# An encoder block with a mixture of experts: router logits with the router's weights as the stationary side, token numbers inside the first expert product, masks on GpSimd

## What is computed

```python
h = rms_norm(x, norm1_g);  z = h @ w_in
mix = sigmoid(gate_a) * (gla(z) @ w_branch_gla) + sigmoid(gate_b) * (dsa(z) @ w_branch_dsa)
x = x + mix @ w_out
t = rms_norm(x, norm2_g)
g_prob = softmax(t @ w_rg + b_rg)                 # 4 groups
g_idx, g_w = argmax(g_prob), max(g_prob)
e_prob = softmax((t @ w_re + b_re)[experts of group g_idx])    # 8 of 32 experts
top_p, top_e = top_k(e_prob, 2)
top_w = g_w * top_p / sum(top_p)
y = 0
for e in range(32):
    y += gate[:, e] * ((silu(t @ w_gate[e]) * (t @ w_up[e])) @ w_down[e])   # 1024 -> 512 -> 1024
x = x + y
```

## Time and profile before

| | us |
|---|---|
| median of 3 runs | 1090.42 (1088.92 to 1090.57) |
| profiled execution | 1090.6 |
| its span, first to last instruction | 1088.8 |
| TensorE busy | 1067.8 (98%) |
| VectorE / ScalarE / GpSimd busy | 550.8 / 344.0 / 289.8 |
| HBM read / written | 262.33 MB / 4.20 MB |
| mean granted TensorE clock | 1.0 of full speed |

### The profile page before, as it was taken

The page is one execution under the profiler, slowest core; times in us unless marked ns, Lnnn a source line. Parts: engine busy times, 40 slices in busy tenths (PEclk is TensorE's granted clock), DMA queues, the critical chain, the costliest instruction groups (busy, mean ns, idle before and its releaser), DMA issues.

```text
span 1088.8 us, 13007 instructions
## 1 busy us (share of the span) xinstructions
PE 1067.8 (98%) x5078; PEld 681.4 (63%) x5078; DVE 550.8 (51%) x1030; ACT 344.0 (32%) x620; POOL 289.8 (27%) x196
## 2 busy tenths in 40 slices
PE   7999999999999999999999999999999999998998
PEld 6777888777788888888888853333333333333333
DVE  5533895699850422339992453333444444442434
ACT  6356632445442554541233311111111111111111
POOL 6733344455551544443523110000000000000000
PEclk9999999999999999999999999999999999999999
DMA  8613333224151222254359989999999999999994
GB/s 214 161 40 78 78 78 78 62 74 116 30 143 39 65 74 58 60 186 126 94 217 370 343 352 402 424 426 424 424 423 426 426 425 423 424 426 425 426 420 199
DMA packets 125935, 263.39 MB, mean 242 GB/s; under 512 B 11953, under 2 KB 97969, under 8 KB 109489
## 3 DMA queue, kind: packets, MB, share of 16 engines
q1 hardware_dynamic: 122128, 255.75, 63.1%
q0 software_dynamic: 2352, 4.18, 1.1%
q10 hardware_dynamic: 1392, 2.62, 0.6%
HBM read 262.33 MB, written 4.20 MB: 245 GB/s over the span
## 4 chain that ended last, share of the span: by engine, by line
PE 96%; DMA 2%; issue 1%; ACT 1%; DVE 0%; SPq 0%; POOL 0%; ACTq 0%; POOLq 0%
PE bank L1138 21%; PE bank L685 19%; PE bank L704 14%; PE bank L1152 11%; PE bank L940 8%; PE bank L1031 4%; PE bank L1158 3%; PE bank L1159 3%; PE bank L912 2%; PE bank L895 2%; PE bank L1125 1%; PE bank L1144 1%; PE bank L903 1%; PE bank L780 1%; PE bank L842 1%
## 5 line engine op out<-in xcount | busy, mean ns | idle before, releaser
L2154 POOL TENSOR_TENSOR piece_r<-arena,piece_r 128x1024 fp32r<-128x1024 f32 x84 | 202.5, 2418 | 242.6 <-ACT piece_r L1294 242.3
L1138 PE MATMUL bank<-arena,work 128*64 128x512 f32 x1024 | 226.7, 595 | 1.2 <-issue 1.2
L685 PE MATMUL bank<-piece_r 128*128 128x512 f32 (+1 forms) x936 | 218.6, 389 | 0.0
L685 PEld LDWEIGHTS bank<-piece_r 128*128 128x128 f32 x936 | 172.5, 188 | 35.9 <-issue 3.5
L1138 PEld LDWEIGHTS bank<-arena,work 128*64 128x64 f32 x1024 | 72.9, 137 | 138.3 <-issue 138.3
L704 PE MATMUL bank<-piece_r 128*128 128x512 f32 x672 | 155.8, 391 | 0.5 <-ACT piece_r L1294 0.5
L704 PEld LDWEIGHTS bank<-piece_r 128*128 128x128 f32 x672 | 125.3, 188 | 29.2 <-issue 3.5
L2012 DVE TENSOR_TENSOR arena<-bank,arena 128x512 f32<-128x512 f32 x126 | 80.9, 685 | 103.5 <-PE bank L1159 103.1
L1294 ACT ACTIVATE piece_r<-arena 128x1024 fp32r<-128x1024 f32 x83 | 87.5, 1057 | 94.9 <-DMA arena<-w_branch_gla_in 49.4
L2268 POOL DMA_INDIRECT arena<-x_rows,idx_pair x15 | 15.2, 1011 | 330.2 <-PE bank L1125 314.5
L2037 DVE SCALAR_TENSOR_TENSOR bias<-bank,slot_sc,bias 128x256 f32<-128x256 f32 x32 | 15.5, 484 | 156.3 <-ACT bias L1537 156.3
(11 more groups left out here) (275 smaller groups left out, 1158.9 us busy)
## 6 DMA issues: line engine op xcount, KB each, us to landing
arena<-w_exp_gate_in SPq DMA_DIRECT2D x28, 2048.0 KB, 26.5
arena<-w_exp_up_in SPq DMA_DIRECT2D x27, 2048.0 KB, 22.4
arena<-w_exp_down_in SPq DMA_DIRECT2D x18, 2048.0 KB, 29.4
arena<-w_in_in SPq DMA_DIRECT2D x68, 512.0 KB, 4.5
wdn_spare<-w_exp_down_in SPq DMA_DIRECT2D x9, 2048.0 KB, 30.9
arena<-w_exp_up_in SPq DMA_DIRECT2D x8, 1024.0 KB, 10.4
arena<-w_exp_gate_in SPq DMA_DIRECT2D x6, 1024.0 KB, 23.2
arena<-w_exp_down_in SPq DMA_DIRECT2D x5, 1024.0 KB, 9.5
```

The lines of the kernel that those rows point to most:

```text
L685: last = mm(bank[n % 2][:, cols], w[:, k, :], h[:, k, cols], start=(i == 0 and k == 0), stop=(i == 2 and k == K - 1))
L1138: last = mm(onto[hf * WIDE:(hf + 1) * WIDE, :], hTe[q][:, k, :], both[:, :, k, hf * HALF:(hf + 1) * HALF], start=(k == 0), stop=(k == K - 1))
L2154: Q.tensor_tensor(quarter(w_lo, q), quarter(w_raw, q), quarter(w_hi, q).bitcast(F32), ALU.subtract).then_inc(s["wlo_ready"], 1)
```

## The change

1. **Router logits.** The router's weights, padded to 64 columns (`wr_wide`), become the stationary side and 128 tokens move; products of even and odd k go to the lower and the upper 64 rows of bank 3. ScalarE copies the 128x128 result to `lgT`, and one product with `fold` (ones at two places a column) adds the two halves and turns them back (`fold_logits`). `lg_ps` and `h2_rs` now count two steps a tile. GpSimd makes `fold` and `wr_wide`, behind a wait for all of mix, and TensorE waits for it ahead of the output product.
2. **Order on TensorE.** The folds are put between passes and parts of `first_rows(0)`; `x2_transposes(3, 1)` moves behind fold(2).
3. **Token numbers.** `tokens_of_slots` moves from ahead of product(0) into its middle; `tok_of` moves to another place in memory, so `load_down_half(0, 1)` no longer waits for `idx_ps`.
4. **Quarters.** The last `first_rows` says when its first half is done; VectorE evicts that quarter (expert 0, k 0 to 3) and product(0) begins on it. `idx_pair` moves behind the slot scales' inputs on VectorE.
5. **Masks.** GpSimd makes the `in_slot` masks of tiles 0 to 2 from the ranks; VectorE makes those of tile 3.
6. **Loads.** Gate and up of expert 5 come in two lots each; the first ones are issued in the middle of product(2).

```diff
-        tok_of = m2(2560, T * TOP_E * NE).rearrange(...)
+        tok_of = piece(9, words=T * TOP_E * NE, off=1024).rearrange(...)
+        wr_wide = m2(512, K * WIDE).rearrange("p (k n) -> p k n", k=K)
+        lgT = [m2(1024 + P * t, P) for t in range(T)]
@@ block.sync
-            sp.wait_ge(s["lg_ps"], T)
+            sp.wait_ge(s["lg_ps"], 2 * T)
             load_down_half(1, 1)
             sp.wait_ge(s["xg_T"], 1)
-            sp.wait_ge(s["idx_ps"], 1)
             load_down_half(0, 1)
...
+                if e == 5:
+                    sp.wait_ge(s["gu_part"], 5)
+                    load(R + 4, CHUNKS[1])
+                    load(R + 5, CHUNKS[1])
+                    sp.wait_ge(s["gu_ready"], 3)
+                    load(R + 4, CHUNKS[2])
+                    load(R + 5, CHUNKS[2])
@@ block.tensor
-                    last = mm(bank[3][:, 0:G + NE], x2T[:, k, t * P:(t + 1) * P], wr[:, k, :],
-                              start=(k == 0), stop=(k == K - 1))
+                    rows = slice(k % 2 * WIDE, (k % 2 + 1) * WIDE)
+                    last = mm(bank[3][rows, 0:P], wr_wide[:, k, :], x2T[:, k, t * P:(t + 1) * P],
+                              start=(k < 2), stop=(k >= K - 2))
+            def fold_logits(t):
+                pe.wait_ge(s["h2_rs"], 2 * t + 1)
+                mm(bank[3][:, LOGITS], lgT[t], fold[:, :], start=True, stop=True).then_inc(s["lg_ps"], 1)
...
-            pe.wait_ge(s["small_w_ready"], 1)
+            pe.wait_ge(s["small_w_ready"], 3)
...
             both_logits(T - 2)
+            first_rows(0, range(2))
+            fold_logits(T - 2)
+            x2_transposes(T - 1, 1)
             ranks(T - 3)
-            x2_transposes(T - 1, 1)
-            first_rows(0, range(4))
+            first_rows(0, range(2, 4))
             both_logits(T - 1)
+            first_rows(0, range(4, 6))
+            fold_logits(T - 1)
+            first_rows(0, range(6, K))
             ranks(T - 2)
-            first_rows(0, range(4, K))
...
-            product(0)
+            for u in range(2):
+                pe.wait_ge(wgu_loaded[u], wgu_loads(u))
+            pe.wait_ge(s["last_sel_ready"], 2)
+            gate_up(product_bank(0), both_of(0)[0], 0, s["gu_ready"], (2, 4), ks=range(4))
+            pe.wait_ge(s["placed"], T)
+            pe.wait_ge(s["sel_ready"], T - 1)
+            for t in range(T):
+                tokens_of_slots(t)
+            pe.wait_ge(s["he_ready"], 1)
+            gate_up(product_bank(0), both_of(0)[0], 0, s["gu_ready"], (6,), ks=range(4, K))
@@ block.scalar
                 mean_square_of_x2(t, 1)
+                act.wait_ge(s["lg_ps"], 2 * t + 1)
+                A(lgT[t], bank[3][:, 0:P], ACT.Copy).then_inc(s["h2_rs"], 1)
                 root_of_x2(t)
@@ block.vector
-                dve.wait_ge(s["h2_rs"], t + 1)
+                dve.wait_ge(s["h2_rs"], 2 * t + 2)
...
+            dve.wait_ge(s["counts_ready"], 2)
+            evict_quarter(0, 0, g2c).then_inc(s["last_sel_ready"], 1)
+            dve.wait_ge(s["xg_T"], 1)
+            evict_quarter(0, 1, g2c).then_inc(s["he_ready"], 1)
+            evict_gathered(1, s["he_ready"], g2c)
@@ block.gpsimd
+            pool.wait_ge(s["mix_ready"], K)
+            for half in range(2):
+                step(Q.tensor_copy(fold[half * WIDE:(half + 1) * WIDE, :],
+                                   ident[half * WIDE:(half + 1) * WIDE, half * WIDE:half * WIDE + G + NE]))
+            step(Q.memset(wr_wide[:, :, G + NE:WIDE], 0.0))
+            Q.tensor_copy(wr_wide[:, :, 0:G + NE], wr[:, :, :]).then_inc(s["small_w_ready"], 1)
...
                 pool.wait_ge(s["placed"], t + 1)
+                for k in range(TOP_E):
+                    st.did(Q.tensor_scalar(in_slot[:, t, k, :], slot_no[:, :], rk[:, k, t:t + 1], None, ALU.is_equal))
+                st.settle()
```

More of the change, by code:

```diff
@@ L310, in encoder_block @@
         entry = sb("entry", [P, TOP_E, T, 2], I32)
+        fold = sb("fold", [P, G + NE])
         eio = sb("eio", [P, NE])
@@ L1067, in _ @@
             both_logits(0)
-            out_pass(T + 1, HIGH, range(K))
+            out_pass(T + 1, HIGH, FRONT)
+            fold_logits(0)
+            out_pass(T + 1, HIGH, BACK)
             out_pass(T + 2, HIGH, FRONT)
@@ L1074, in _ @@
             out_pass(T + 3, HIGH, FRONT)
+            fold_logits(1)
             x2_transposes(2, 1)
@@ L1107, in _ @@
             last.then_inc(s["counts_ready"], 1)
-            first_rows(T - 1)
-            pe.wait_ge(s["placed"], T)
-            for t in range(T):
-                tokens_of_slots(t)
+            first_rows(T - 1, range(4))
+            first_rows(T - 1, range(4, K))
             def slot_scales():
@@ L1128, in gather_transposes, with gate_up @@
                     last.then_inc(done, 1)
-            def gate_up(onto, both, q, done, parts=(), second_lot=None):
-                for k in range(K):
-                    if k in parts:
-                        last.then_inc(s["gu_part"], 1)
+            def gate_up(onto, both, q, done, parts=(), second_lot=None, ks=range(K)):
+                for k in ks:
                     if k == K // 2 and second_lot is not None:
@@ L1139, in gate_up @@
                                   both[:, :, k, hf * HALF:(hf + 1) * HALF], start=(k == 0), stop=(k == K - 1))
-                last.then_inc(done, 1)
+                    if k + 1 in parts:
+                        last.then_inc(s["gu_part"], 1)
+                if K - 1 in ks:
+                    last.then_inc(done, 1)
             def hidden_transposes(done):
@@ L1932, in _ @@
             place(T - 1)
-            for q in range(2):
-                dve.wait_ge(s["xg_T"], 1)
-                evict_gathered(q, s["he_ready"], g2c)
-                if q == 0:
-                    dve.wait_ge(s["idx_ps"], 1)
-                    V.tensor_scalar(idx_pair[:, :], bank[1][:, 0:PAIRS_E], float(S), None, ALU.add)\
-                        .then_inc(s["idx_ready"], 1)
+            dve.wait_ge(s["counts_ready"], 2)
[3 more added lines that the diff above has]
+            evict_gathered(1, s["he_ready"], g2c)
             st.did(V.tensor_tensor(rsg[:, :, :, 0, :], oh,
@@ L1955, in _ @@
                 .then_inc(s["rsg_ready"], 1)
+            dve.wait_ge(s["idx_ps"], 1)
+            V.tensor_scalar(idx_pair[:, :], bank[1][:, 0:PAIRS_E], float(S), None, ALU.add)\
+                .then_inc(s["idx_ready"], 1)
             st.did(V.tensor_scalar(tok_pair[:, 0, :], bank[1][:, 0:PAIRS_E], float(S), None, ALU.add))
@@ L2271, in gather @@
                     bounds_check=S - 1, oob_is_err=False).then_inc(done, 16)
-            pool.wait_ge(s["lg_ps"], T)
+            pool.wait_ge(s["lg_ps"], 2 * T)
             for p in range(1, PAIRS_E):
```

44 lines of the change are left out of this document (24 added, 20 removed).

## The result

| | before | changed |
|---|---|---|
| median | 1090.29 | **1096.70** (1095.42 to 1096.83) |
| ratio of the medians, 95% interval | | 1.0056 [1.0043, 1.0069] |
| span of the profiled execution | 1088.8 | 1094.9 |
| mean granted TensorE clock | 1.0 | 0.998 |

The forecast was 1092.6, with a range up to 1096.0. The sign was right; the time came out 4.1 us longer and outside the range.

The account below looks back on a forecast made before the run. Weight arrival by DMA was taken to bound the kernel. Front +3.7, router stage +0.4 and queue -1.9 gave +2.2 us on 1090.4, forecasting 1092.6 us; the range was 1089.0 to 1096.0.

Parts of the forecast that it names:

- Which bound holds: Expert stage: weight arrival by DMA sets the end; TensorE has 6.3 us of slack, so its gain alone buys nothing.
- The 4.1 us of waits: Near the kernel's end: TensorE, itself 4.1 us late, was to keep 4.1 of its 6.3 us of waits for weights.
- Front of the output product, +3.7: First output matmul waits for mix and four GpSimd steps, starting about 571.6 instead of 567.92; range 3.3 to 4.5 us.
- a rival with 12%: Output product: TensorE's clock falls during the new 3.5 us wait, adding 2.5 us, in all 1095.1; chance 12%.
- Router stage, +0.4 (-0.3 to +1.2): Logits to last first_rows: 3.1 us less TensorE work, but the chain through the engines ends it 0.4 us later.
- my third item: Router stage: fold(2), queued behind first_rows(0, range(2)) and GpSimd's selection, makes choose_group(2) start about 0.5 us later.
- The rival that TensorE's 3.1 us would be won: Router stage: bound by TensorE's work, not the chain, so 3.1 us are saved in full, total 1089.1; chance 15%.
- a change between array modes adds a drain: Router logits between wide products make eight mode changes; by the skill's rule some tenths in all, by the row none.
- First product and lots, -1.9 (1.0 to 2.4): Weights' queue around product(0) and expert 5: earlier load_down_half(0, 1) and two lots gain 1.9 us against first_rows.
- the queue's margin is 1.8: Weights' queue after product(2): of a 2.4 us lead, only 1.8 us is usable before it runs dry again.
- a sign of being wrong: Expert stage: a DMA rate below 400 GB/s again after 668 us would show the forecast wrong.
- the later gather: First gather, issued about 5 us behind first_rows instead of 2.1, lands at +14.5, before TensorE asks at +16.1.

Follow-up runs that it names:

- Run 3: Kernel before with only a TensorE wait for all of mix ahead of the output product: 1093.61 us, ratio 1.0033.
- run 4: Kernel before with only expert 5's gate and up loads in two lots, the first issued in the middle of product(2): 1089.11 us, ratio 0.9994.
- runs 1: Changed kernel with TensorE's wait for the wide router weights moved from ahead of the output product to ahead of the first logits: 1090.83 us, ratio 1.0005.
- run 8: Changed kernel with twelve 128 by 128 identity products on TensorE ahead of its new wait, filling idle time: 1094.99 us, ratio 1.0036.
- run 2: Changed kernel with GpSimd's two copies into fold made ahead of its wait for mix: 1096.09 us, ratio 1.0053.
- run 5: Changed kernel with the wait moved ahead of the first logits and the masks of tiles 0 to 2 back on VectorE: 1090.51 us, ratio 1.0003.
- run 9: Changed kernel with the wait ahead of the first logits and tile 2's fold moved ahead of first_rows(0, range(2)): 1090.98 us, ratio 1.0004.
- run 6: Kernel before with token numbers inside product(0), quarter evictions and two lots for expert 5; logits, masks and front as before: 1088.88 us, ratio 0.9982.
- run 10: Kernel before with token numbers inside product(0), quarters and two lots for expert 5, plus two lots for expert 6: 1088.93 us, ratio 0.9988.

## Why the prediction was wrong

**Which bound holds.** Right. Run 3 moves F and W by one amount, run 4 moves W alone by a change of the loads, and TensorE's last stops stay (0.70 at 1039.63). The 4.1 us of waits that I said would be left is wrong by my own sum: 6.3 less the 1.9 that the queue gains is 4.4. Six stops from 990 us on, 4.9 together, were left.

**Front of the output product, +3.7.** The step that failed. Its first part was mis-sized: 4.1, since the two 36-column copies took 0.44 each for 0.13. I had costed them by their columns from one cast of 1024; the row of the small memset said nothing of a copy. Its second part was taken as a rival with 12%: the clock does fall in the stop. It cost 1.7 us (runs 1 and 8) for the 2.5 worked out. The argument against it, that the one fall in the trace of before came after 3.8 us, was no bound at all: it said only that 3.8 is enough. In run 2 the clock fell with a stop of 3.07. The Trainium skill (TensorE: Matmul & The Clock Gate, HAM oscillation) warns of idle gaps of about the length of the 3.95, and the trace agrees. The falls with 3.07 and with about 2 us (last section) are shorter than the gaps that this section warns of, so there the traces go further than the page. I should have given this rival far more than 12%.

**Router stage, +0.4 (-0.3 to +1.2).** Outside its bounds: +1.5. TensorE's and ScalarE's durations were nearly right (1.09 with the drain for 0.87, which by the two rows should have been 0.90; the copy 0.28). What failed is the chain from a tile's logits to VectorE, by which tile 3's were to come 0.13 late; they come 0.99 late against A (40.62, before 39.63). Timeline of VectorE before, then of TensorE and VectorE in the changed kernel:

```profile
616.52 0.22 DVE L1848 SCALAR_TENSOR_TENSOR lg<-bank,rs,router_b 128x4 f32<-128x4 f32 x1 [0.68 <-PE bank L986]
```
```profile
621.10 1.09 PE L998 MATMUL bank<-arena,work 128*64 128x128 f32 x16
...
622.17 1.17 PE L1047 MATMUL bank<-piece_r 128*128 128x512 f32 x4
623.17 0.30 PE L1006 MATMUL bank<-fold,work 128*128 128x36 f32 x2
```
```profile
623.59 0.22 DVE L1881 SCALAR_TENSOR_TENSOR lg<-bank,rs,router_b 128x4 f32<-128x4 f32 x1 [0.69 <-PE bank L1006]
```

Before, tile 1's logits are taken 1.98 us after their first product starts (614.54); now 2.49 after (621.10), since the copy, four output matmuls and the fold lie between. Another 0.45 is already there when tile 1's logits begin, 0.37 of it from tile 0: the copy has to wait 0.69 for the logits, and the table load, VectorE's group choice and the addition ahead of tile 1's transposes stand behind it (TensorE waits 0.59 there; I had 0.2 for this addition). The lateness is 0.96 at tile 1, 1.58 at tile 2, where VectorE waits 1.50 for the fold behind `first_rows`, and 0.99 at tile 3. This 1.0 is the new logits' own, as run 5 shows with the masks away (46.35 for 45.34). The masks add 0.5 (0.46 each; I took 0.2 and had 0.41 as the high end), between tile 3's logits and F: 6.24 us for 5.71. The fold of tile 2 behind `first_rows`, my third item, costs nothing by itself (run 9). The rival that TensorE's 3.1 us would be won is refuted: the stage is bound by the chain. That a change between array modes adds a drain is not seen in any row.

**First product and lots, -1.9 (1.0 to 2.4).** Right in kind, near in size: 1.6 gained in the changed kernel, 1.25 in runs 1, 4 and 6, 1.4 in runs 5 and 9, 0.7 in run 8, so one execution tells it to some tenths only. `load_down_half(0, 1)` went out 1.1 earlier as forecast. But with the old logits the lots alone (run 4) win as much as lots and product part together (run 6): a part of the 1.1 is lost again within 10 us behind F, which I had not foreseen, and a part at the next hole, as I had. That the queue's margin is 1.8 is not borne out, since run 10 closes that hole of 0.7 and wins 0.4. The new hole at 686 (352 GB/s) is what I had named as a sign of being wrong. Token numbers inside the product and the later gather cost nothing seen.

**The sum**: 0.3 (stages ahead) + 4.1 + 1.7 + 1.5 - 1.6 = 6.0, in place of 3.7 + 0.4 - 1.9 = 2.2. Of the 3.8 missing, the clock is 1.7, the router stage 1.1, the stop 0.4, and the rest 0.6 the queue and the stages ahead. Three of these were independent, and a range that took in each rival alone (1096.0) did not hold two of them together.

## What to carry to other kernels

A wait belongs in front of the first instruction that needs it: one line put TensorE's first consumer of a late tile where its user was 40 us away, and it alone made a change of no effect into a loss of 0.6%. Where a stop in front of dense matmuls is to be priced, price the clock with it, and take a fall that was seen after a longer stop as no evidence against one after a shorter. Fewer TensorE microseconds buy nothing in a stage that is a chain through four engines; follow one tile through all of them first.

## What the runs showed that I had not expected

**The length of the late stop does not tell whether the clock falls.** In all 13 profiled executions TensorE stops once for about 2 us (1.77 to 2.67) between 990 and 1011 us, and in 6 of them the clock falls. Most often a down product stands behind it (16 matmuls, 3.65 us at full clock) and shows the clock. The timelines of run 9 and then of run 2:

```profile
1004.31 5.35 PE L1175 MATMUL bank<-arena,bias 128*64 128x512 f32 x16 [1.97 <-issue]
```
```profile
1010.08 5.35 PE L1174 MATMUL bank<-arena,bias 128*64 128x512 f32 x16 [1.77 <-issue]
```

After 1.97 and 1.77 us it ran at half clock for a time (5.35), yet after 2.26 us in the kernel before it took 3.65, and after the 2.22 us at the front of run 3 the clock stayed at 1.00. What tells the two cases apart is open. Such a fall near the end costs 1.7 us of TensorE's slack and not the end: in run 9 the last wait is still there, 0.29 us long, and in run 2 it is gone. At the front, where nothing has slack, the same 1.7 us are paid in full.

**A small GpSimd operation has a price of its own.** 64 x 36 copied takes 0.44 us, 128 x 64 compared 0.46, and 128 x 288 copied 0.42: between these sizes the columns hardly count. Only the memsets were cheaper, 0.28 for 128 x 224 and 0.14 for 64 x 64.
